# Low parts of the FFN weights moved from GpSimd to VectorE, two PSUM copies to ScalarE, and three bank pairs in the opening, in a three-layer float32 transformer kernel

## What is computed

```python
f = (jax.nn.silu(h @ w_gate[l]) * (h @ w_up[l])) @ w_down[l]      # layer 1
gate, up = jnp.split(h @ w_in, 2, axis=-1)                         # layers 2 and 3
return (jax.nn.silu(gate) * up) @ w_out
```

## Time and profile before

| | us |
|---|---|
| median of 3 runs | 2017.98 |
| the profiled execution | 2017.78 |
| its span | 2016.0 |
| TensorE busy | 1956.5 (97%) |
| VectorE busy | 1172.7 (58%) |
| ScalarE busy | 873.5 (43%) |
| GpSimd busy | 663.5 (33%) |

### The profile page before, as it was taken

The page is one execution under the profiler, slowest core; times in us unless marked ns, Lnnn a source line. Parts: engine busy times, 40 slices in busy tenths (PEclk is TensorE's granted clock), DMA queues, the critical chain, the costliest instruction groups (busy, mean ns, idle before and its releaser), DMA issues.

```text
span 2016.0 us, 28330 instructions
## 1 busy us (share of the span) xinstructions
PE 1956.5 (97%) x9919; PEld 1635.1 (81%) x9919; DVE 1172.7 (58%) x1628; ACT 873.5 (43%) x1251; POOL 663.5 (33%) x259
## 2 busy tenths in 40 slices
PE   9999989999999999999999999999999999999999
PEld 6777778887888888888878888888777777888787
DVE  5765776767137456454277776324778777676600
ACT  6664533334234444434343334225888643232411
POOL 3233331214423334343442123443222243122443
PEclk9999989999999999999999999999999999999999
DMA  5212123222323222222332222322111132322222
GB/s 174 67 63 94 58 100 104 85 71 97 100 85 102 76 94 88 68 94 73 105 125 84 94 83 75 100 96 83 63 52 62 51 115 86 110 88 73 87 97 98
DMA packets 49023, 177.53 MB, mean 88 GB/s; under 512 B 5568, under 2 KB 6464, under 8 KB 48960
## 3 DMA queue, kind: packets, MB, share of 16 engines
q1 hardware_dynamic: 39744, 147.78, 22.2%
q10 hardware_dynamic: 9216, 28.91, 4.2%
HBM read 174.57 MB, written 2.10 MB: 88 GB/s over the span
## 4 chain that ended last, share of the span: by engine, by line
PE 73%; DVE 17%; DMA 5%; issue 3%; ACT 1%; DVEq 1%; ACTq 1%; SPq 0%
PE B L393 16%; PE B L394 16%; PE B L402 15%; DMA R<-in_w_seven 4%; DVE S L2216 3%; DVE HD L2165 2%; PE B L845 2%; DVE SL L2224 2%; PE B L849 2%; PE B L847 2%; DVE ML L2280 2%; PE B L1367 2%; PE B L414 1%; PE B L1175 1%; PE B L419 1%
## 5 line engine op out<-in xcount | busy, mean ns | idle before, releaser
L645 POOL TENSOR_TENSOR WL<-RAW,WH 128x1024 fp32r<-128x1024 f32 (+1 forms) x248 | 652.5, 2633 | 1324.9 <-PE B L402 835.5
L374 ACT CAST WH<-RAW 128x1024 fp32r<-128x1024 f32 (+1 forms) x252 | 278.6, 1107 | 636.0 <-PE B L394 558.5
L393 PE MATMUL B<-HH,WH 128*128 128x512 f32 x1224 | 482.1, 394 | 11.0 <-ACT WH L374 6.2
L394 PE MATMUL B<-HL,WH 128*128 128x512 f32 x1224 | 479.2, 392 | 0.0
L402 PE MATMUL B<-HH,WL 128*128 128x512 f32 x1224 | 304.8, 391 | 0.0
L393 PEld LDWEIGHTS B<-HH,WH 128*128 128x128 f32 x1224 | 231.2, 189 | 61.9 <-issue 8.7
L394 PEld LDWEIGHTS B<-HL,WH 128*128 128x128 f32 x1224 | 231.2, 189 | 46.3
L402 PEld LDWEIGHTS B<-HH,WL 128*128 128x128 f32 x1224 | 226.3, 188 | 45.6 <-POOL WL L645 0.4
L393 PE MATMUL B<-MH,WH 128*128 128x512 f32 x440 | 171.2, 389 | 0.0
L394 PE MATMUL B<-ML,WH 128*128 128x512 f32 x440 | 171.2, 389 | 0.0
L2328 DVE TENSOR_TENSOR X<-X,B 128x512 f32 x26 | 17.9, 687 | 206.7 <-PE B L402 192.9
(11 more groups left out here) (434 smaller groups left out, 3636.3 us busy)
## 6 DMA issues: line engine op xcount, KB each, us to landing
RAW<-in_w_small SPq DMA_DIRECT2D x206, 512.0 KB, 3.4
RAW<-in_w_large SPq DMA_DIRECT2D x48, 704.0 KB, 4.0
SUMS<-in_w_seven ACTq DMA_DIRECT2D x24, 512.0 KB, 4.0
R<-in_w_seven ACTq DMA_DIRECT2D x24, 512.0 KB, 4.8
out_t<-X SPq DMA_DIRECT2D x7, 256.0 KB, 5.1
X<-in_x_t ACTq DMA_DIRECT2D x4, 256.0 KB, 6.0
X<-in_x_t SPq DMA_DIRECT2D x4, 256.0 KB, 6.3
DECAY<-in_decay ACTq DMA_DIRECT2D x4, 256.0 KB, 2.6
```

The lines of the kernel that those rows point to most:

```text
L374: act.copy(wh, raw).then_inc(s_hi, 1)
L393: pe.matmul(bank, wh[:, c, :], xh[:, k0 + c, :], start=(start and c == 0), stop=False)
L394: mm = pe.matmul(bank, wh[:, c, :], xl[:, k0 + c, :], start=False, stop=False)
L645: pool.tensor_tensor(wl, raw, wh.bitcast(F32), ALU.subtract).then_inc(s_lo, 1)
```

## The change

- GpSimd makes no low part from unit 4 of an FFN to its last (24 units); it waits until they are counted. VectorE makes them (`weights`), two in each iteration, each ahead of its own `low_part`.
- In `seven` ScalarE copies b to GS and c_ to US; VectorE adds a and subtracts a. Low parts of Q4, Q3, Q6 and Q5 move to the start of the iteration that uses them, with the previous pair's up and hidden tile behind the first two.
- ScalarE loads R when Q4's low part is done and LANDED_1 after its copy of b. Its cast of the next gate weights stays ahead of the copy of a (CW) that Q5 waits for.
- Opening: layers 2 and 3 use the bank pairs (0, 1), (2, 3), (4, 5), (0, 1), layer 1's last up goes to B1. ScalarE loads the first blocks earlier; casts are reordered.
- Tail: hidden tiles in smaller groups around the scalings and the low parts.

```diff
         t_kept = sem("seven_partial_kept")
-        t_c11 = sem("seven_gate_first_half")
+        t_second = sem("seven_second_product_kept")
+        t_seventh = sem("seven_seventh_product_kept")
+        t_first_half = sem("seven_gate_first_half_scaled")
         t_silu = sem("seven_silu_done")
-        t_up = sem("seven_up_added")
         t_up_scaled = sem("seven_up_scaled")
...
 first = 0
-cuts = [(U_OUT1 + 6, DC), (U_FFN1 + 4 - U_OUT1 - 6, DC), (U_DOWN1 - U_FFN1 - 4, DC), (14, HALF), (2, HALF), (6, DC)]
-stretches = cuts + [(STRETCHES[2][0] - 6, DC), (U_SB - U_DOWN2, HALF), (2, DC), (U_LAST - U_SB - 2, DC),
-                    (U_DOWN3 - U_LAST, DC), (U_END - U_DOWN3, HALF)]
+by_vector = 2 * NC - 4
+cuts = [(U_OUT1 + 6, DC), (U_FFN1 + 4 - U_OUT1 - 6, DC), (by_vector, 0), (14, HALF), (2, HALF), (6, DC)]
+stretches = cuts + [(U_FFN2 + 4 - U_RET - 6, DC), (by_vector, 0), (U_SB - U_DOWN2, HALF), (2, DC),
+                    (U_LAST - U_SB - 2, DC), (U_FFN3 + 4 - U_LAST, DC), (by_vector, 0),
+                    (U_END - U_DOWN3, HALF)]
 for count, chunks in stretches:
+    if not chunks:
+        first += count
+        pool.wait_ge(s_lo, first)
+        continue
     start = 0
...
         use_unit(pe, Unit(u0 + 6), B[2][:], DC, HH, HL)
-        pe.wait_ge(s_up, 1)
-        use_unit(pe, Unit(u0 + 7), B[3][:], DC, HH, HL)
+        pe.wait_ge(s_up, PRO - 1)
+        use_unit(pe, Unit(u0 + 7), B[1][:], DC, HH, HL)
     else:
         pair(0, before)
-        for n in range(1, PRO):
-            pair(n)
+        pe.wait_ge(s_gate, NC * f + 1)
+        for n, bank in ((1, 2), (2, 4), (3, 0)):
+            if n == 3:
+                pe.wait_ge(s_up, NC * f + 1)
+            use_unit(pe, Unit(u0 + 2 * n), B[bank][:], DC, HH, HL)
+            use_unit(pe, Unit(u0 + 2 * n + 1), B[bank + 1][:], DC, HH, HL)
...
-        pe.wait_ge(t_lo, i * 6 + (lo0 + 3))
+        pe.wait_ge(t_lo, i * 6 + (lo0 + 5))
         pe.wait_ge(t_bank, i * 4 + (bank0 + 5))
...
-        pe.wait_ge(t_lo, i * 6 + (lo0 + 4))
+        pe.wait_ge(t_lo, i * 6 + (lo0 + 6))
         pe.wait_ge(t_kept, i + (NS * f + 1))
...
-        pe.wait_ge(t_lo, i * 6 + (lo0 + 5))
         pe.wait_ge(t_bank, i * 4 + (bank0 + 6))
         product(Q3, HH, HL, lower, SECOND, a)
-        pe.wait_ge(t_lo, i * 6 + (lo0 + 6))
         product(Q4, TH, TL, T4, every, c_)
...
     pe.wait_ge(t_input_lo, 4 * (f + 1))
+    pe.wait_ge(s_up, NC * f + PRO - 1)
     with pe.Fori(0, NS) as i:
...
         ahead = i + 1
+        act.wait_ge(t_lo, i * 6 + (6 * group0 + 3))
         if produce:
-            products_done(i, 2)
-            act.wait_ge(t_lo, i * 6 + 6 * (group0 + 1))
-            load(i + (group0 + 1))
+            act.dma_start(R[:], blocks[i * 2 + (2 * group0 + 3)]).then_inc(t_landed_2, 16)
+        products_done(i, 2)
+        act.copy(GS[:, FIRST], B[5][:, FIRST]).then_inc(t_second, 1)
+        if produce:
+            act.dma_start(LANDED_1, blocks[i * 2 + (2 * group0 + 2)]).then_inc(t_landed_1, 16)
+        products_done(i, 3)
+        act.copy(US[:, SECOND], B[6][:, FIRST]).then_inc(t_seventh, 1)
         split_hi(act, Unit(u0 + 2 * PRO + 2, i, 2), DC)
-        if produce:
-            singles_hi(ahead)
         products_done(i, 4)
...
         if produce:
+            singles_hi(ahead)
             sum_7_hi(ahead)
...
         split_hi(act, Unit(u0 + 2 * PRO + 3, i, 2), DC)
+        if produce:
+            products_done(i, 6)
+            sum_3_hi(ahead)
         act.wait_ge(t_bank, i * 4 + ((4 * NS + 4) * f + 7))
...
         if produce:
-            products_done(i, 6)
-            sum_3_hi(ahead)
             products_done(i, 7)
...
     input_block()
+    load(group0)
     pair(1, DC, splits[1])
-    load(group0)
     input_sums_hi()
     pair(2, DC, splits[2])
-    for hi in (singles_hi, sum_7_hi, sum_6_hi, sum_5_hi, sum_3_hi, single_4_hi):
+    singles_hi(0)
+    split_hi(act, Unit(u0 + 2, 3, 2), DC)
+    for hi in (sum_7_hi, sum_6_hi, sum_5_hi, sum_3_hi, single_4_hi):
         hi(0)
-    pair(3, DC, splits[3])
+    silu(3)
+    split_hi(act, Unit(u0 + 3, 3, 2), DC)
     with act.Fori(0, NS - 1) as i:
...
     products_done(NS - 1, 7)
-    pair(NC - 2, DC, between=lambda: some_hidden(range(0, 10)))
-    some_hidden(range(10, 14))
-    pair(NC - 1, chunks_after, between=lambda: some_hidden(range(14, EARLY)))
-    some_hidden(range(EARLY, FC))
+    some_hidden(range(0, 5))
+    pair(NC - 2, DC, between=lambda: some_hidden(range(5, 9)))
+    some_hidden(range(9, 12))
+    pair(NC - 1, chunks_after, between=lambda: some_hidden(range(12, 19)))
+    some_hidden(range(19, FC))
...
-    a, b, c_ = B[4][:, FIRST], B[5][:, FIRST], B[6][:, FIRST]
+    a, c_ = B[4][:, FIRST], B[6][:, FIRST]
+
+    def weights(u):
+        dve.wait_ge(s_hi, u.index + 1)
+        dve.wait_ge(s_unit, u.index - 1)
+        raw, wh, wl = place(u)
+        dve.tensor_tensor(wl, raw, wh.bitcast(F32), ALU.subtract).then_inc(s_lo, 1)
...
         ahead = i + 1
-        products_done(i, 2)
-        dve.tensor_copy(GS[:, FIRST], a).then_inc(t_c11, 1)
-        dve.wait_ge(t_c11, i * 2 + (2 * group0 + 1))
-        dve.tensor_tensor(GS[:, FIRST], GS[:, FIRST], b, ALU.add).then_inc(t_bank, 1)
+        lo(i, 6, Q4, A22)
+        lo(i, 5, Q3, S3[:])
+        up_and_hidden(i + (PRO - 1), B[1][:])
+        dve.wait_ge(t_second, i + (group0 + 1))
+        dve.tensor_tensor(GS[:, FIRST], GS[:, FIRST], a, ALU.add).then_inc(t_bank, 1)
+        lo(i, 3, Q6, s6)
+        weights(Unit(u0 + 2 * PRO, i, 2))
         dve.wait_ge(t_bank, i * 4 + ((4 * NS + 4) * f + 5))
-        dve.tensor_tensor(GS[:, FIRST], GS[:, FIRST], RB[:, FIRST], ALU.mult).then_inc(t_c11, 1)
+        dve.tensor_tensor(GS[:, FIRST], GS[:, FIRST], RB[:, FIRST], ALU.mult).then_inc(t_first_half, 1)
+        lo(i, 4, Q5, s5)
+        weights(Unit(u0 + 2 * PRO + 1, i, 2))
         if produce:
...
             sum_3(ahead)
+        gate_scaled(i + PRO, B[0][:])
+        if produce:
             low_singles(ahead)
-            lo(ahead, 2, Q7, s7)
-        gate_scaled(i + PRO, B[0][:])
         products_done(i, 5)
-        dve.wait_ge(t_kept, i + (group0 + 1))
-        dve.tensor_copy(US[:, SECOND], c_).then_inc(t_up, 1)
-        dve.wait_ge(t_up, i + (group0 + 1))
+        dve.wait_ge(t_seventh, i + (group0 + 1))
         dve.tensor_tensor(US[:, SECOND], US[:, SECOND], a, ALU.subtract).then_inc(t_bank, 1)
...
             minus_sum_5()
-            lo(ahead, 3, Q6, s6)
-            lo(ahead, 4, Q5, s5)
+            lo(ahead, 2, Q7, s7)
         products_done(i, 6)
...
         dve.wait_ge(t_hidden, i + (group0 + 1))
-        up_and_hidden(i + PRO, B[1][:])
-        if produce:
-            lo(ahead, 5, Q3, S3[:])
-            lo(ahead, 6, Q4, A22)
...
-    banks = list(banks) + [(0, 1)] * (PRO - len(banks))
-
-    def opening_pair(n):
-        gate, up = banks[n]
-        pair(n, B[gate][:], B[up][:])
-
-    opening_pair(0)
+    banks = banks or ((0, 1), (2, 3), (4, 5), (0, 1))
+
+    def opening_gate(n):
+        gate_scaled(n, B[banks[n][0]][:])
+
+    def opening_up(n):
+        up_and_hidden(n, B[banks[n][1]][:])
+
+    opening_gate(0)
+    opening_up(0)
     input_sums()
-    opening_pair(1)
+    opening_gate(1)
+    dve.wait_ge(s_lo, u0 + 4)
+    weights(Unit(u0 + 4))
+    opening_up(1)
+    weights(Unit(u0 + 5))
     input_sums_lo()
-    opening_pair(2)
+    opening_gate(2)
+    weights(Unit(u0 + 6))
+    opening_up(2)
+    dve.sem_inc(t_bank, 4)
     sum_7(0)
...
     minus_sum_5()
+    weights(Unit(u0 + 7))
     low_singles(0)
     lo(0, 2, Q7, s7)
-    lo(0, 3, Q6, s6)
-    lo(0, 4, Q5, s5)
-    lo(0, 5, Q3, S3[:])
-    lo(0, 6, Q4, A22)
-    opening_pair(3)
-    dve.sem_inc(t_bank, 4)
+    opening_gate(3)
     with dve.Fori(0, NS - 1) as i:
...
     seven(NS - 1, produce=False)
+    end = u0 + 2 * (NC - 2)
+    weights(Unit(end))
+    up_and_hidden(NC - 3, B[1][:])
+    weights(Unit(end + 1))
+    some_hidden(range(0, 5))
     gate_scaled(NC - 2, B[0][:])
-    some_hidden(range(0, 5))
+    weights(Unit(end + 2))
+    some_hidden(range(5, 9))
     up_and_hidden(NC - 2, B[1][:])
-    some_hidden(range(5, 14))
+    weights(Unit(end + 3))
+    some_hidden(range(9, 12))
     gate_scaled(NC - 1, B[0][:])
-    some_hidden(range(14, 18))
+    some_hidden(range(12, 19))
     up_and_hidden(NC - 1, B[1][:])
-    some_hidden(range(18, FC))
+    some_hidden(range(19, FC))
...
 rnorm(2)
-ffn(0, U_FFN1, ((2, 3), (4, 5), (0, 1), (2, 3)))
+ffn(0, U_FFN1, ((2, 3), (4, 5), (0, 1), (2, 1)))
 outputs(1, 3, U_DOWN1, 2, True)
...
```

## The result

The changed kernel takes 1958.21 us (median; 1957.22 to 1959.37), 0.9705 of the kernel before (95% interval 0.9688 to 0.9722), where 1956.0 was predicted. The profiled execution took 1958.58 us, span 1956.8, mean clock 0.997.

The account below looks back on a forecast made before the run. TensorE, busy 97% of the span, was taken as the bound, leaving only pauses and slow stretches to win: 2017.78 - 39.3 (loops) - 13.3 (openings) - 10.1 (tails) = 1955.1, with 0.9 allowed 1956.0 us; range 1950 to 1976.

Parts of the forecast that it names:

- Loops: Eight seven-product iterations in each of three FFNs: each loop falls from about 181 to 168.3 us, 39.3 us won.
- the chain low part → RAW[0] → cast → CW: In each loop iteration, gate's low part frees RAW[0] for load, cast and copy before Q5: 0.4 us to spare.
- rival A: In the loops, the cast chain ends late and Q5 waits every iteration: 14 us, 1970 in all; chance 0.14.
- Rival B: VectorE becomes the bound in the loops, or the openings break: 1979, or 1990 with old pauses; chance 0.08.
- The lock: Skill's exclusive lock of a port VectorE shares with GpSimd: S3's sum takes 2.78 us instead of 0.69 in the loops.
- the crossing: In the loops, GpSimd's low part runs beside VectorE's two-input work and holds it: S3's sum 2.78 us, not 0.69.
- R's late load: In the loops, VectorE waited 4.31 us for R, which was loaded only after the last low part.
- Rival D: Pauses have another cause, such as R's load, which stays; half the loop term goes: 1975; chance 0.06.
- Openings 2 and 3 and the starts of the down projections: Second and third FFN openings without pauses, 5.0 and 6.4 us won; no half-clock start of down projections, 3.3 us.
- First opening: First FFN before its loop: one long pause replaces three short ones, Q1 at 270.7 against 272.65, 1.9 us won.
- the clock: After the first opening's long pause, TensorE runs at half speed for 3 us, losing 1.5 us.
- Tails: Last two plain pairs of each FFN: 24.02, 24.00 and 24.10 us fall to 21.77 each, 6.8 us won.

Follow-up runs that it names:

- late gate weights: The changed kernel with VectorE making gate's low part after gate's scaling and Q5's low part; 1975.17 us, 0.9785 of the kernel before.
- CW first: The changed kernel with ScalarE's copy CW put ahead of its cast of the next gate weights; 1955.26 us, 0.9671 of the kernel before.

## Why the prediction was right, step by step

The sum expected 62.7 us before the allowance of 0.9; 59.2 came.

- **Loops**: 39.3 expected; 544.17 went to 508.31, 35.9 won. This term holds the whole miss. 24 x 21.04 = 504.96, and the 3.3 over it are the six long iterations (0.89 + 0.81 + 0.67 + 0.61 + 0.18 + 0.13). The failed step is the chain low part → RAW[0] → cast → CW. Its parts were right (load out at 6.1 us against 5.95, cast 1.05), but the landing was taken as 3.4 with 0.4 to spare: in the eighteen iterations without a wait it took 3.29 to 3.57 us, in the six with one 3.62 to 4.52. The real margin was 0.1 to 0.2. The bounds of 3.4 to 4.0 rested on LANDED_1 landing at 7.6, before RAW's data move, and that is where they broke: in the four iterations with a landing of 3.98 or more LANDED_1 landed 7.52 to 7.77 us after Q1, in the others at 7.38 or before. That is rival A's mechanism, in 6 iterations of 24; late gate weights and CW first show it from both sides.
- **VectorE** has 110.35 / 8 = 13.8 us of work per iteration against 13.3 expected, and its WL takes 1.22. Rival B falls. The advice of the Trainium skill (Perfetto Trace Analysis, Optimizing Scalar/DVE Operations) is for a saturated VectorE, and at 58% it was none: the engine took the work and its busy share fell to 57%. Nor did the move of the low parts bring anything in the total: GpSimd with the new order gives the same 1958, by terms that cancel.
- **The lock** of the Trainium skill (SBUF — State Buffer, Who interferes with whom): the traces agree, with 1.79 to 2.93 us for forms of 0.69 to 1.22 us that read two inputs from SBUF and start 0.1 to 1.2 us behind GpSimd's low part, and their own time without it. Of itself it cost nothing where the order leaves 2 us behind it.
- **Both reasons given for VectorE's lateness stand**, the crossing and R's late load. The crossing is shown by its removal, which also let R land 1.7 us sooner; by the estimate there the crossing alone would just have been enough. R's landing is shown only by the length of the old iterations, which follows it, since sending R earlier in the old order didn't make it land earlier. (The 4.0 us taken for R from the earlier trace rows are LANDED_1's; R took 4.8 before and 3.4 in the changed kernel, where it lands 5.1 to 5.4 us after Q1 in the inner iterations.) Rival D didn't come: R's load didn't stay where it was. How much of the new order's gain is the blocks' earlier landing and how much the shorter queue ahead of the subtraction isn't separated.
- **Openings 2 and 3 and the starts of the down projections**: 5.0 + 6.4 + 3.3 = 14.7 expected. From tail end to Q1 the times fell from 570.48 to 565.18 and from 432.16 to 423.96, from the last tail's end to the end of the span from 124.4 to 122.6: 15.2 won. That no pause would be left was right, and the margins held (units 4 to 7 of the second FFN are 2.9, 5.6, 4.4 and 3.3 us early, 2.9, 5, 4 and 3.5 laid out); the credit given to the bank pairs was wrong, VectorE's order and its free low parts do it alone.
- **First opening**: 1.9 expected, 1.2 came (Q1 at 271.43 against 270.7). The pause ended at 250.72 (250.6 laid out) and unit 6 was cast at 254.25 (254.2). The mis-sized part is the clock: half speed for 5.3 us, where 3 us were taken from the old trace; 12 starts x 0.2 = 2.4 us lost instead of 1.5. The longer pause isn't shown to be the reason: with GpSimd making all low parts, a pause of 3.77 us in the same place was followed by 5.7 us at half speed, and one of 3.80 before the change by 3.4.
- **Tails**: 24.02 + 24.00 + 24.10 went to 3 x 21.76, 6.8 won, as laid out.

## What to carry to other kernels

When a wait shows two causes in a row, remove each alone before paying for both: here either the order or the crossing sufficed. When an edit is meant to bring data earlier, look at the landing and not at the issue, and at every iteration and not at one: R left 0.8 us earlier and landed when it did before. On an in-order engine, put nothing that waits for a DMA ahead of a short copy with a deadline; a margin of 0.1 to 0.2 us under a load whose landing varies by 1 is a wait in every fourth iteration. Time won upstream arrives only if the next thin place is widened with it: 2 and 3 us alone, 12 together.

## What the runs showed of the hardware

- RAW's 512 KB for the next gate took 3.3 to 3.7 us from issue to landing in 20 iterations of the changed kernel and 3.98 to 4.52 in four. Those are the four in which the block load ahead of it, LANDED_1, landed latest (7.5 us after Q1 and later, with RAW out at 5.8 to 6.3). With gate's low part late, where RAW went out 0.94 us later, none of 24 took over 3.63, with LANDED_1 landing as late as 8.06. Why the block load is late at times is open.
- The half-clock stretch behind a pause was 5.3 us after 10.5 us of idle, and 3.4 and 5.7 us after 3.8 us of idle in two kernels: the length of the pause doesn't tell it.
- GpSimd's low part holds whichever instruction with two inputs in SBUF VectorE starts next: with S3's sum out of its way, the low part behind the sum took 3.2 us instead of 1.23. One that reads a bank isn't held: up's scaling (U<-B,RB), started 0.23 us behind GpSimd in the kernel before, took its 0.69.
